# mLSTM of a two-block transformer: queries weighed ahead, local and inter products summed in one PSUM place, squares at the end of a head

## The reference

```
w_inter = exp(a_inter - m_t)
s   = exp(d - m_t) * (q . k)
num = w_inter * (C . q) + s @ v
den = w_inter * (n . q) + sum(s)
h   = num / max(|den|, exp(-m_t))
C_new, n_new = decay * (C, n) + sum(wg * v k, wg * k)
```

## Time and profile before

| what | value |
|---|---|
| median of 3 runs | 3360.27 us (3358.48 to 3361.23) |
| the profiled execution | 3358.81 us, its span 3356.9 us |
| TensorE busy | 3240.3 us, mean granted clock 0.975 |
| mLSTM, first product to first maximum of the attention | 1082.4 to 1202.55 us of the span |

### The profile page before, as it was taken

The page is one execution under the profiler, slowest core; times in us unless marked ns, Lnnn a source line. Parts: engine busy times, 40 slices in busy tenths (PEclk is TensorE's granted clock), DMA queues, the critical chain, the costliest instruction groups (busy, mean ns, idle before and its releaser), DMA issues. The chain is left out here.

```text
span 3356.9 us, 39728 instructions
## 1 busy us (share of the span) xinstructions
PE 3240.3 (97%) x16070; PEld 2702.5 (81%) x16070; DVE 2018.5 (60%) x2589; ACT 1325.1 (39%) x2011; POOL 441.8 (13%) x495
## 2 busy tenths in 40 slices
PE   7999999999999799999999999979999999999998
PEld 5788888878787679878888888867879887787987
DVE  6556556544763788665565555555238876425885
ACT  4222222233334368532222222362128854213872
POOL 0010110112011113110110111001102400100330
PEclk8999999999999789999999999989999999999999
DMA  5222222226355279312222222224426612445451
GB/s 203 88 90 75 88 88 76 88 74 115 107 181 175 73 132 117 86 38 76 101 88 88 88 76 88 70 62 125 129 80 81 98 39 74 144 125 80 60 92 63
DMA packets 140726, 320.70 MB, mean 96 GB/s; under 512 B 55824, under 2 KB 72976, under 8 KB 129536
## 3 DMA queue, kind: packets, MB, share of 16 engines
q1 hardware_dynamic: 86000, 232.48, 24.7%
q0 software_dynamic: 54544, 85.68, 10.9%
HBM read 261.52 MB, written 51.10 MB: 93 GB/s over the span
## 5 line engine op out<-in xcount | busy, mean ns | idle before, releaser
L2163 DVE TENSOR_TENSOR w_lo<-w_raw,w_hi 128x1024 fp32r<-128x1024 f32 (+1 forms) x126 | 210.4, 1670 | 310.2 <-ACT w_hi L1564 310.2
L898 PE MATMUL psum<-a_hi,w_hi 128*128 128x512 f32 x704 | 276.5, 393 | 5.9 <-DVE a_lo L2308 3.8
L898 PE MATMUL psum<-a_hi,w_lo 128*128 128x512 f32 x704 | 275.2, 391 | 0.0
L898 PE MATMUL psum<-a_lo,w_hi 128*128 128x512 f32 x704 | 275.0, 391 | 0.0
L2661 DVE TENSOR_TENSOR attn_tl<-psum,attn_th 128x512 fp32r<-128x512 f32 x384 | 246.2, 682 | 5.6 <-ACT attn_th L1911 4.4
L2376 DVE SCALAR_TENSOR_TENSOR x<-psum,cols,x 128x1024 f32<-128x1024 f32 x144 | 184.4, 1282 | 93.5 <-PE psum L898 93.2
L1911 ACT ACTIVATE attn_th<-psum 128x512 fp32r<-128x512 f32 x384 | 209.5, 598 | 67.3 <-PE psum L1306 62.9
L1564 ACT ACTIVATE w_hi<-w_raw 128x1024 fp32r<-128x1024 f32 (+1 forms) x126 | 174.2, 1383 | 123.1 <-PE psum L898 39.6
L1306 PEld LDWEIGHTS psum<-mats,attn_num 128*128 128x128 f32 x1536 | 178.9, 141 | 34.6 <-issue 8.6
L1306 PE MATMUL psum<-mats,attn_num 128*128 128x128 f32 x1536 | 201.4, 274 | 5.2 <-DVE attn_tl L2661 5.0
L3322 POOL TENSOR_TENSOR sq<-w_raw 128x256 f32<-128x256 f32 x40 | 29.7, 742 | 1165.9 <-DMA w_raw<-in_w_gu 1155.1
(11 more groups left out here) (581 smaller groups left out, 8465.1 us busy)
## 6 DMA issues: line engine op xcount, KB each, us to landing
w_raw<-in_w_ada SPq DMA_DIRECT2D x52, 1024.0 KB, 5.0
w_raw<-in_w_gu SPq DMA_DIRECT2D x44, 1024.0 KB, 4.9
w_raw<-in_w_in SPq DMA_DIRECT2D x34, 1024.0 KB, 5.2
w_raw<-in_w_down SPq DMA_DIRECT2D x22, 1024.0 KB, 5.0
w_raw<-in_w_out SPq DMA_DIRECT2D x12, 1024.0 KB, 6.8
qk_hi_scratch<-p_out_hi POOLq DMA_DIRECT2D x18, 512.0 KB, 3.0
qk_lo_scratch<-p_out_lo POOLq DMA_DIRECT2D x18, 512.0 KB, 3.8
w_early<-in_w_ada SPq DMA_DIRECT2D x8, 1024.0 KB, 18.2
```

Source lines behind the costliest of these rows:

```text
L898: mm = e.matmul(bank, a[:, k * width + m * P:k * width + (m + 1) * P], b(k, h), start=(ends[0] and k == order[0] and i == 0), stop=(ends[1 ...
L2163: e.tensor_tensor(like(src, lo), src, like(src, hi.bitcast(F32)), ALU.subtract).then_inc(*w_done.mark(n, part))
```

## The change

The inter weights move from the result to the query. The rows w_inter, which ScalarE has already computed in `QA`, are stored to DRAM and read back as rows broadcast to the 64 partitions of a head; queries times these rows give `qw`, by VectorE for head 0 and by GpSimd for heads 1 to 3. Local and inter products then accumulate in the same PSUM place. VectorE's weighing and sum go, `num` goes; Abs, the multiplication and the sum into hs read PSUM. ScalarE's squares move from the norm step (in the next head's loop, behind the weighted keys and exponentials) to the end of `ml_outputs`. Memory is rearranged for the two `qw` tiles, and signals are added for the new events.

```diff
 TensorE, ml_outputs
             for dr in range(2):
                 for c0 in (0, 4):
-                    pl = ps.take(e, ("ml l", h, dr, c0), ml_dve, "num", h, dr, c0)
+                    p = ps.take(e, ("ml l", h, dr, c0), ml_dve, "h", h, dr, c0)
                     e.wait_ge(*ml_dve.at("S", h, dr))
...
-                    pi = ps.take(e, ("ml i", h, dr, c0), ml_dve, "inter", h, dr, c0)
                     e.wait_ge(*ml_dve.at("C", h, 4, dr))
+                    e.wait_ge(*(ml_scaled.at(h, dr) if h else ml_dve.at("weighed", dr)))
                     for c in range(c0, c0 + 4):
                         j = c if dr == 0 else ST - 1 - c
+                        to = p.full[:, (c % 4) * 256:(c % 4) * 256 + M_V + 1]
+                        local = e.matmul(to, m.E[i][dr][:, c, :], m.v1[c // 4][:, c % 4, h, :], start=True, stop=False)
+                        inter = e.matmul(to, m.qw[dr][part, c * P:(c + 1) * P], m.C[part, dr, j, :], start=False, stop=True)
...
 ScalarE
+        def ml_squares(h):
...
+            for f in range(2):
+                e.wait_ge(*ml_dve.at("h", h, 1, 4))
+                if h:
+                    e.wait_ge(*ml_dve.at("ss", h - 1, f))
+                e.activation(sqh[f].rearrange("p (c v) -> p c v", c=4), m.hs[i][:, 4 * f:4 * f + 4, :],
+                             ACT.Square).then_inc(*ml_act.mark("square", h, f))
         def ml_outputs(h):
...
-                    e.wait_ge(*ml_dve.at("num", h, dr, c0))
-                    e.activation(de[:, 0:4].unsqueeze(2), nu[:, :, M_V:M_V + 1], ACT.Abs).then_inc(*ml_act.mark("abs", h, dr, c0))
+                    e.wait_ge(*ml_pe.at("i", h, dr, c0))
+                    if dr:
+                        e.wait_ge(*ml_dve.at("h", h, 0, c0))
...
+                    e.activation(m.dn[n % 2][:, 0:4].unsqueeze(2), sums, ACT.Abs).then_inc(*ml_act.mark("abs", h, dr, c0))
                     n += 1
+                    if (dr, c0) == (1, 4):
+                        ml_squares(h)
 VectorE, ml_prepare, after each masking of scores
+                if h == 0:
+                    e.wait_ge(*ml_qk[0].at(0))
+                    e.wait_ge(*ml_w_in[dr].at(0))
+                    e.tensor_tensor(m.qw[dr][part, :], m.qw[dr][part, :], m.qk[0][part, :], ALU.mult).then_inc(
+                        *ml_dve.mark("weighed", dr))
 VectorE, ml_outputs
-                    e.tensor_tensor(nu[:], pi3, m.colsA[:, c0:c0 + 4, 64 + row:64 + row + 1].to_broadcast([P, 4, M_V + 1]),
-                                    ALU.mult).then_inc(*ml_dve.mark("inter", h, dr, c0))
-                    e.wait_ge(*ml_dve.now())
-                    e.tensor_tensor(nu[:], nu[:], pl3, ALU.add).then_inc(*ml_dve.mark("num", h, dr, c0))
...
-                        e.tensor_tensor(dst, nu[:, :, 0:M_V], rb, ALU.mult).then_inc(*ml_dve.mark("h", h))
+                        e.tensor_tensor(dst, p3[:, :, 0:M_V], de[:, 8:12].unsqueeze(2).to_broadcast([P, 4, M_V]),
+                                        ALU.mult).then_inc(*ml_dve.mark("h", h, dr, c0))
                     else:
-                        e.tensor_tensor(nu[:, :, 0:M_V], nu[:, :, 0:M_V], rb, ALU.mult).then_inc(*ml_dve.mark("back", h))
-                        e.wait_ge(*ml_dve.now())
-                        e.tensor_tensor(dst, dst, nu[:, :, 0:M_V], ALU.add).then_inc(*ml_dve.mark("h", h))
+                        for c in range(4):
+                            e.scalar_tensor_tensor(out=dst[:, c, :], in0=p3[:, c, 0:M_V], scalar=de[:, 8 + c:9 + c],
+                                                   in1=dst[:, c, :], op0=ALU.mult, op1=ALU.add).then_inc(
+                                *ml_dve.mark("h", h, dr, c0))
 GpSimd
                 e.wait_ge(*minus_M_in[2 + dr if h else dr].at(h))
+                if h >= 2:
+                    e.wait_ge(*ml_scaled.now())
...
+        def weigh_queries(h):
+            m, part = t.ml, slice(64 * (h % 2), 64 * (h % 2) + 64)
+            e.wait_ge(*ml_qk[h // 2].at(h // 2))
+            e.wait_ge(*ml_masked.now())
+            for dr in range(2):
+                e.wait_ge(*ml_w_in[2 * (h % 2) + dr].at(h))
+                e.tensor_tensor(m.qw[dr][part, :], m.qw[dr][part, :], m.qk[h // 2][part, :], ALU.mult).then_inc(
+                    *ml_scaled.mark(h, dr))
...
             causal(1)
+            weigh_queries(1)
             for h in range(M_HEADS - 1):
                 if h + 2 < M_HEADS:
                     causal(h + 2)
+                    weigh_queries(h + 2)
 SyncE
+            def inter_rows(h):
+                part = slice(64 * (h % 2), 64 * (h % 2) + 64)
+                for dr in range(2):
+                    if h >= 2:
+                        e.wait_ge(*ml_pe.at("i", h - 2, dr, 4))
+                    e.dma_start(m.qw[dr][part, :], d.ml_w[32 * dr + h].unsqueeze(0).to_broadcast([64, S])).then_inc(
+                        *ml_w_in[2 * (h % 2) + dr].mark(h))
...
+            e.wait_ge(*ml_act.at("rows ready"))
+            e.dma_start(d.ml_w[:, :], t.proj1.QA[64:64 + ROWS, :]).then_inc(*w_stored.mark())
             p1b_stored("tile", 9, 0)
...
             e.dma_start(m.qk[0][:], d.proj[8]).then_inc(*ml_qk[0].mark(0))
+            inter_rows(0)
             for dr in range(2):
                 minus_M(m.nb[dr], 1, dr, 2 + dr)
+            inter_rows(1)
...
                     minus_M(m.nb[dr], h, dr, 2 + dr)
+                inter_rows(h)
```

More of the change, by code:

```diff
@@ L491, in memory @@
     with ExitStack() as sc:
-        m.qk = [sb(f"ml_{n}", [P, S], F32, sc) for n in ("q0", "q1")] + [None, sb("ml_k1", [P, S], F32, sc)]
+        m.qk = [sb(f"ml_{n}", [P, S], F32, sc) for n in ("q0", "q1")] + [None, None]
         m.C = sb("ml_C", [P, 2, ST, M_V + 1], F32, sc)
         m.nb = rings("ml_minus_M", 2, [P, ST, P], F32, sc)
-        gap("ml_0", 32 * 1024 - 28 * 1024 - 64, sc)
+        m.qw = [sb("ml_qw0", [P, S], F32, sc)]
+        m.qk[3] = sb("ml_k1", [P, S], F32, sc)
         m.ktok = sb("ml_ktok", [P, ST, 256], F32, sc)
@@ L499, in memory @@
         m.v1 = rings("ml_v", 2, [P, 4, M_HEADS, M_V + 1], F32, sc)
-        m.num = rings("ml_num", 2, [P, 4, M_V + 1], F32, sc)
-        gap("ml_1", 65 * 1024 + 512 - 60 * 1024 - 128 - 4 * 1024 - 32, sc)
+        m.qw.append(sb("ml_qw1", [P, S], F32, sc))
+        gap("ml_1", 65 * 1024 + 512 - 60 * 1024 - 4 * 1024 - 192, sc)
         m.E = [[sb(f"ml_E0{d}", [P, ST, P], F32, sc) for d in range(2)]]
@@ L675, in program_of @@
     x_turned, z_turned = signal("x_turned", "PE"), signal("z_turned", "PE")
-    ml_masked, w_sums = (signal(n, "Pool") for n in ("ml_masked", "w_sums"))
+    ml_masked, w_sums, ml_scaled = (signal(n, "Pool") for n in ("ml_masked", "w_sums", "ml_scaled"))
     cs_done, w_hi, squared, guessed = (signal(n, "ACT") for n in ("cs_done", "w_hi", "squared", "guessed"))
@@ L1245, in ml_outputs @@
             part = slice(lo, lo + 64)
-            qt = m.qk[pr]
             for dr in range(2):
                 for c0 in (0, 4):
-                    pl = ps.take(e, ("ml l", h, dr, c0), ml_dve, "num", h, dr, c0)
+                    p = ps.take(e, ("ml l", h, dr, c0), ml_dve, "h", h, dr, c0)
                     e.wait_ge(*ml_dve.at("S", h, dr))
[L1251 to L1254, removed]
-                    pi = ps.take(e, ("ml i", h, dr, c0), ml_dve, "inter", h, dr, c0)
                     e.wait_ge(*ml_dve.at("C", h, 4, dr))
+                    e.wait_ge(*(ml_scaled.at(h, dr) if h else ml_dve.at("weighed", dr)))
                     for c in range(c0, c0 + 4):
                         j = c if dr == 0 else ST - 1 - c
-                        mm = e.matmul(pi.full[:, (c % 4) * 256:(c % 4) * 256 + M_V + 1], qt[part, c * P:(c + 1) * P],
-                                      m.C[part, dr, j, :], start=True, stop=True)
-                    mm.then_inc(*ml_pe.mark("i", h, dr, c0))
+                        to = p.full[:, (c % 4) * 256:(c % 4) * 256 + M_V + 1]
+                        local = e.matmul(to, m.E[i][dr][:, c, :], m.v1[c // 4][:, c % 4, h, :], start=True, stop=False)
+                        inter = e.matmul(to, m.qw[dr][part, c * P:(c + 1) * P], m.C[part, dr, j, :], start=False, stop=True)
+                    local.then_inc(*ml_pe.mark("l", h, dr, c0))
+                    inter.then_inc(*ml_pe.mark("i", h, dr, c0))
                     yield
@@ L1856, in ml_outputs @@
                 for c0 in (0, 4):
[L1857 to L1859 removed]
+                    sums = ps.of[("ml l", h, dr, c0)].full.rearrange("p (c v) -> p c v", c=4)[:, :, M_V:M_V + 1]
+                    e.wait_ge(*ml_pe.at("i", h, dr, c0))
+                    if dr:
+                        e.wait_ge(*ml_dve.at("h", h, 0, c0))
+                    elif h:
+                        e.wait_ge(*ml_dve.at("h", h - 1, 1, c0))
+                    e.activation(m.dn[n % 2][:, 0:4].unsqueeze(2), sums, ACT.Abs).then_inc(*ml_act.mark("abs", h, dr, c0))
                     n += 1
+                    if (dr, c0) == (1, 4):
+                        ml_squares(h)
                     yield
```

(6 more changed lines are left out.)

7 lines of the change are left out of this document (6 added, 1 removed).

## The result

The kernel after takes **3373.6 us** (median of 5, 3369.86 to 3375.03), beside 3361.23 (3358.48 to 3363.71) for the kernel before in the same comparison: ratio 1.0034, 95% interval 1.0024 to 1.0045. It is 12 us slower, where I had forecast 9 faster, and it lies outside my range.

The account below looks back on a forecast made before the run. TensorE bounds the whole run, but VectorE's order of work paces it in the mLSTM. Terms along that chain, 2.5 - 3.2 + 2.1 - 4.4 - 5.6 = -8.6 us, take the median 3360.3 to 3351.7 us; range 3342 to 3362.

Parts of the forecast that it names:

- the term for TensorE's products: Local and inter products in the mLSTM: taking turns costs 0, between nothing and 0.93 us per tile.
- TensorE's stands: Heads 1 to 3: TensorE's waits for PSUM places go, 3.2, 4.4 and 2.7 us earlier.
- Waits beside GpSimd: Head 0: maxima of the first three tiles wait 5.0 us beside GpSimd where it was 1.3, 3.7 more.
- second rival: Head 2: GpSimd also holds VectorE's small one-SBUF-operand operations, the mean losing 6.4 us; 3358.1 us, chance 0.27.
- third rival: Three heads: maxima wait through GpSimd's rows of four additions, 22.0 us more instead of 3.7; 3370 us, chance 0.11.
- first rival: Head 3: with fewer stands TensorE runs at 2.4 GHz, 7.4 us less; 3344.3 us, chance 0.18.
- DMA: Head 0: four row broadcasts of 256 KB join full DMA engines and delay the chain by 2.4 us.
- VectorE's work: mLSTM stage, 1082 to the first attention maximum: VectorE's work of 93 us falls by about 23.
- alternated products slower than 2.09 us for eight: Sign of being wrong: turn-taking local and inter products take over 2.09 us per group of eight.
- a first Abs after 1106: Sign of being wrong, head 0: the first Abs comes after 1106 us for want of the mask.
- no stand over 1 us in heads 1 and 2: Sign of being right: TensorE never stands over 1 us for a PSUM place in heads 1 and 2.
- the first attention maximum: Sign of being right, end of the mLSTM: VectorE's first maximum of the attention comes near 1194 us.

Follow-up runs that it names:

- e5: Kernel after, with each tile's products ordered two local, four inter, two local, so two changes of row count per tile; 3357.66 us, ratio 0.9995 to before.
- e3: Kernel after, with each local product over one half of its 128 rows, so all turn-taking products have 64 rows; 3360.36 us in one execution.
- e9: e5 with ScalarE's outputs step (Abs, squares) ahead of the next head's preparation in each round; 3356.16 us, ratio 0.9991 to the kernel before.
- e13: e5 with plain queries, without any weighing, its loads or multiplications (result lacks the factor w); 3354.66 us, ratio 0.9981 to the kernel before.
- e12: Kernel before, with only ScalarE's squares moved to the end of a head's outputs; 3362.80 us, ratio 1.0004.

## Why the prediction was wrong

**The step that failed** is the term for TensorE's products, which stands outside the chain of the sum: "TensorE's products stay the same in number and size; no row shows local and inter products taking turns, and I take 0, between nothing and 0.93 us per tile". The term is 5.78 - 4.01 = 1.77 us per tile at 1.2 GHz and about 1.2 at 2.4 GHz (3.35 against 2 x 1.09, the step from a group of eight to the next in the trace of before), both above the upper end: six more changes of shape per tile, at 0.30 and 0.20 us each. Over 16 tiles TensorE's work in the stage grew by 25.9 us (118.42 - 92.56), and putting the order right gives back 13 of the 20 us, by the ratios, between forecast and result. I had bounded it from a row that has nothing to do with it, the eight products at either clock level. The nearer row was in the trace: the weight load of the first inter product stood 0.23 us behind the local ones. Eight such changes per tile instead of two, at that 0.23 us, give 6 x 0.23 = 1.4 us per tile at 1.2 GHz, 22 us in all if every tile ran so, and with it the other sign.

The Trainium skill, "TensorEngine Tiling (Array Packing)", section "Tiling Modes", says that changing the tiling mode, and not just the tile, drains TensorE. By that rule each change between 128*128 and 64*128 products, as the rows write them, costs; the traces agree (0.23 us of standing at each change of shape at 1.2 GHz, from 128*128 to 128*64 in e5 as well, and none between products of one shape in e3). It was the rule to look for, since it speaks against this change; the page gives no duration, the trace did.

**TensorE's stands** (heads 1 to 3; 3.2, 4.4 and 2.7 us of gain in the sum). Head 1's three stands are gone, but one of 1.59 us for hs has come there; head 2 had 3.37 and 1.03 us and now has 3.89 and 1.04. The sentence "that is under 2 us, with three other places to go to; so TensorE's three stands go" was wrong. hs waits for an Abs, the first Abs of head 0 is queued behind 16 exponentials, and these wait for the mask: the place of head 0's first tile is held from 1096.03 until 1106.60 in the kernel after. In e5, where TensorE is fast again, it stands 7.17, 1.99, 2.56 and 3.89 us for hs. These stands, which the sum had struck out, are the likeliest place of the remaining 7 us (-8.6 forecast, -1.7 in e5), and about 2 may be the changes of shape that e5 keeps. That is argued, not shown: e9 removes the longest stand and wins only 1.3 us, and e13 keeps 4.53 and 3.89 us without any weighing. How the 7 us divide the runs can't settle, as differences of 1 to 3 us lie within their intervals.

**Waits beside GpSimd.** Maxima: I placed 5.0 us of waiting at the first three tiles; 2.20 and 2.22 us came there, and 1.13 in head 2. The second rival's mechanism is real: means of 2.24 us (beside GpSimd's weighing at 1127.19) and 1.42. The trace agrees with what the prediction cites from the Trainium skill, "SBUF — State Buffer", section "Who interferes with whom". Its size was 3.3 us (3.66 less 2 x 0.17), not 6.4, and how much of it lay on the path isn't shown. The third rival's 22 us did not come.

**The clock.** The first rival fell: the granted clock of the last head is 0.53, below the 0.60 of before, although TensorE stands less there.

**DMA.** 2.4 us were taken; GpSimd's wait for the store grew from 7.22 to 9.97, and the first exponential came at 1098.54 instead of 1096.60, 1.9 later. The size fits but isn't shown to be the loads': e13, without them, still waits 8.66 us, and e12 9.02, so single profiles differ by as much as the term.

**VectorE's work** fell by 17.8 us, not 23. The four operations of a backward tile take 1.13 us, near the 1.1 I took. Stalls count as busy time: maxima and means together hold 7.2 us more than before, and the stalled sum of the earlier trace rows took 4.9 with it. That is 2.3 of the 5 us that are missing; the rest I have not traced.

Of the signs of being wrong, "alternated products slower than 2.09 us for eight" is the one that came; "a first Abs after 1106" did not (1103.23). Of the signs of being right, no stand over 1 us in heads 1 and 2 failed (1.59, 3.89, 1.04), and the first attention maximum came at 1217.85, not near 1194.

## What to carry to other kernels

Count the changes of the products' shape (128*128, 64*128, 128*64 in the rows) in TensorE's order before and after an edit, not only products and columns: one change cost 0.30 us at 1.2 GHz and 0.20 at 2.4 GHz here, and the standing before the weight load shows it. Products that add into one PSUM place can be ordered so that kinds stay together: begin one half of the places with the local product and the other half with the inter product. When two places become one, look who frees it now, and what is queued ahead of that on every engine in between.

## What I had not expected of the hardware

Turn-taking products of 128 and 64 rows follow at 0.73 us, turn-taking products of 64 rows at 0.43, both at 1.2 GHz. At 2.4 GHz it is 0.42 against 0.22 (e3 at 1100 us). The difference, 0.30 and 0.20 us per product, falls with the clock but is not halved. At 1.2 GHz the price is the same where the row count stays and only the shape changes, 128*128 to 128*64. And a mean over 8 columns with one SBUF operand took 2.24 us beside a GpSimd product of 2.34.
